# Decay, beta and running-maximum rows repeated over the partitions by GpSimd's transfers instead of by products with the identity

## Time and profile before

| | |
|---|---|
| median of three runs | 1260.62 us (1257.66 to 1260.63) |
| the profiled execution, its own time | 1257.48 us |
| its span, from first to last instruction | 1255.5 us |
| PE busy | 1183.1 us (94%) |
| DVE busy | 314.8 us (25%) |
| ACT busy | 129.1 us (10%) |
| POOL busy | 33.7 us (3%) |
| moved by DMA | 441.27 MB, mean 351 GB/s |
| the chain that ended last, by engine | PE 65%, DMA 31%, DVE 3% |

### The profile page before, as it was taken

The page is one execution under the profiler, slowest core; times in us unless marked ns, Lnnn a source line. Parts: engine busy times, 40 slices in busy tenths (PEclk is TensorE's granted clock), DMA queues, the critical chain, the costliest instruction groups (busy, mean ns, idle before and its releaser), DMA issues.

```text
span 1255.5 us, 13834 instructions
## 1 busy us (share of the span) xinstructions
PE 1183.1 (94%) x5889; PEld 623.5 (50%) x5889; DVE 314.8 (25%) x686; ACT 129.1 (10%) x216; POOL 33.7 (3%) x48
## 2 busy tenths in 40 slices
PE   8999999999999999999899898999999898899986
PEld 6889999985633443434334242434434243434342
DVE  2784325252520211102011110102111010202012
ACT  3551001101000000000000000000000000000001
POOL 3700000000000000000000000000000000000000
PEclk9999999999899999999999999999999999999999
DMA  9933323474699999999999999899999999999993
GB/s 269 328 101 107 105 91 109 176 300 187 253 430 416 428 428 428 427 429 426 427 430 426 428 427 418 360 428 427 429 428 426 428 428 426 429 427 427 429 428 146
DMA packets 61582, 441.27 MB, mean 351 GB/s; under 512 B 8176, under 2 KB 32976, under 8 KB 36848
## 3 DMA queue, kind: packets, MB, share of 16 engines
q1 hardware_dynamic: 57104, 438.38, 85.0%
q10 hardware_dynamic: 4416, 1.99, 0.7%
HBM read 439.30 MB, written 1.05 MB: 351 GB/s over the span
## 4 chain that ended last, share of the span: by engine, by line
PE 65%; DMA 31%; DVE 3%; issue 0%; SPq 0%; ACT 0%; DVEq 0%
DMA ring<-in_w_down 31%; PE bank L805 21%; PE bank L845 14%; PE bank L493 13%; PE bank L509 3%; PE bank L785 3%; PE bank L746 2%; PE bank L882 2%; PE bank L716 1%; PE bank L705 1%; PE bank L797 1%; PE bank L857 1%; PE bank L516 1%; PE bank L579 0%; DVE cvg L1440 0%; PE bank L867 0%
## 5 line engine op out<-in xcount | busy, mean ns | idle before, releaser
L805 PE MATMUL bank<-ring,cvg 128*64 128x512 f32 x2112 | 461.6, 593 | 9.0 <-DMA ring<-in_w_gate_up 8.7
L805 PEld LDWEIGHTS bank<-ring,cvg 128*64 128x64 f32 x2112 | 151.2, 137 | 300.2 <-issue 274.9
L845 PE MATMUL bank<-ring,cvg 128*64 128x512 f32 x1024 | 236.3, 618 | 38.7 <-DMA ring<-in_w_down 38.7
L1450 DVE TENSOR_SCALAR cvm<-bank 128x512 f32<-128x512 f32 x33 | 22.8, 691 | 654.8 <-PE bank L805 654.8
L845 PEld LDWEIGHTS bank<-ring,cvg 128*64 128x64 f32 x1024 | 80.6, 142 | 192.5 <-issue 192.4
L493 PE MATMUL bank<-ring 128*128 128x256 f32 x768 | 171.7, 382 | 0.0
L493 PEld LDWEIGHTS bank<-ring 128*128 128x128 f32 x768 | 145.4, 192 | 19.9 <-issue 0.7
L1801 ACT ACTIVATE cvm<-cvm 128x512 f32<-128x512 f32 x33 | 20.8, 630 | 501.7 <-DVE cvm L1450 501.7
L785 PEld LDWEIGHTS bank<-ltm,hn 128*128 128x128 f32 x544 | 67.8, 199 | 7.1 <-issue 7.1
L785 PE MATMUL bank<-ltm,hn 128*128 128x128 f32 x544 | 67.9, 284 | 0.0
L882 PE MATMUL bank<-vb,ltm 128*128 128x512 f32 x128 | 57.7, 593 | 0.0
(11 more groups left out here) (315 smaller groups left out, 615.1 us busy)
## 6 DMA issues: line engine op xcount, KB each, us to landing
ring<-in_w_gate_up SPq DMA_DIRECT2D x128, 2048.0 KB, 34.6
ring<-in_w_down SPq DMA_DIRECT2D x64, 2048.0 KB, 36.7
ring<-in_w_in SPq DMA_DIRECT2D x24, 1024.0 KB, 6.6
ring<-in_w_out SPq DMA_DIRECT2D x4, 1024.0 KB, 5.0
ring<-in_w_up_ml SPq DMA_DIRECT2D x2, 1024.0 KB, 5.1
ring<-in_w_up_gdn SPq DMA_DIRECT2D x2, 1024.0 KB, 5.0
xs<-in_x SPq DMA_DIRECT2D x2, 512.0 KB, 4.6
out<-hn SPq DMA_DIRECT2D x2, 512.0 KB, 2.7
```

Source lines behind the costliest of these rows:

```text
L805: mm = pe.matmul(B[4 + half][side * SLOTS:(side + 1) * SLOTS, :], xT[:, k, e * SLOTS:(e + 1) * SLOTS], w[:, (k % 2) * PIECE + at:(k % 2) * ...
L845: mm = pe.matmul(B[6 + half][e * SLOTS:(e + 1) * SLOTS, :], actT[:, e, at:at + SLOTS], by_block(double(of[e]), 4)[:, j, half * HALF:(half ...
L1450: dve.tensor_scalar(g2, both[:, :, :, 0], SWIGLU_LIMIT, None, ALU.min).then_inc(sem("glu_g_ready"), 1)
```

## The change

`spread` and its three calls are gone from PE. GpSimd gets a function of four transfers, `share_rows`, between its tables and the splitting of the bias: `rows` and `cmrow` are written to DRAM and read back to all 128 partitions, 8 KB and 4 KB on each. They land in parts of the ring of weights that are not in use then (`spread_rows` where the gates come later, `spread_runmax` where `inv` comes later). DVE reads its three operands there, in SBUF, instead of in PSUM, and waits for the transfers' semaphores.

```diff
--- before.py
+++ after.py
@@ -152,6 +152,10 @@
         cvm = sb("cvm", [P, 2 * HC, S])
         gate_g = ring[:, 9, 0:KC * S].rearrange("p (k s) -> p k s", k=KC)
         gate_m = ring[:, 9, KC * S:2 * KC * S].rearrange("p (k s) -> p k s", k=KC)
+        spread_rows = gate_g.rearrange("p (h b) s -> p h (b s)", b=1)
+        spread_runmax = late[4].rearrange("p (h s) -> p h s", h=H)
+        rows_copy = nc.dram_tensor("rows_copy", [2 * H, S], F32).ap()
+        runmax_copy = nc.dram_tensor("runmax_copy", [H, S], F32).ap()
         z_s, mo_s, mv_s = rows4(late[0]), rows4(late[1]), rows4(late[2])
         decay = mixer_only(T * H * P).rearrange("p (h t i) -> p h t i", h=H, t=T)
         pt = ring[:, 8, KC * S:KC * S + 3 * H * P].rearrange("p (h b i) -> p h b i", h=H, b=3)
@@ -459,6 +463,17 @@
                     link(ins)
             ins.then_inc(sem("tables_ready"), 1)
 
+            def share_rows():
+
+                pool.wait_ge(sem("rows_ready"), 1)
+                pool.dma_start(rows_copy, rows[:, :]).then_inc(sem("rows_kept"), 16)
+                pool.dma_start(runmax_copy, cmrow[:, :]).then_inc(sem("runmax_kept"), 16)
+                pool.wait_ge(sem("rows_kept"), 16)
+                pool.dma_start(spread_rows, rows_copy.partition_broadcast(P)).then_inc(sem("rows_spread"), 16)
+                pool.wait_ge(sem("runmax_kept"), 16)
+                pool.dma_start(spread_runmax, runmax_copy.partition_broadcast(P)).then_inc(sem("runmax_spread"), 16)
+
+            share_rows()
             pool.wait_ge(sem("expert_bias"), 48)
             for i in range(3):
                 own = slice(i * E, (i + 1) * E)
@@ -573,16 +588,6 @@
                 mm = pe.transpose(B[5][:, 480 + t * H:480 + (t + 1) * H], cmrow[:, t * P:(t + 1) * P], ident[0:H, 0:H])
             mm.then_inc(sem("runmax_turned"), 1)
 
-            def spread(src, first, banks, signal):
-                n = src.shape[0]
-                for h in range(H):
-                    mm = pe.matmul(B[banks[h // 2]][:, (h % 2) * S:(h % 2 + 1) * S],
-                                   ident[0:n, first + h:first + h + 1].to_broadcast([n, P]), src[:, :],
-                                   start=True, stop=True)
-                mm.then_inc(sem(signal), 1)
-
-            pe.wait_ge(sem("hT_ready"), 2 * T)
-            spread(rows, 0, (0, 1), "decay_spread")
             proj(4)
 
             pe.wait_ge(sem("squares_ready"), 2)
@@ -593,9 +598,6 @@
             mm.then_inc(sem("norm_sums"), 1)
             proj(5)
             pe.wait_ge(sem("roots_ready"), 2)
-            spread(rows, H, (2, 3), "beta_spread")
-            pe.wait_ge(sem("dmin_ready"), 1)
-            spread(cmrow, 0, (4, 5), "runmax_spread")
             proj(6)
 
             pe.wait_ge(sem("k_normed"), 1)
@@ -1146,10 +1148,10 @@
                                          op1=ALU.mult).then_inc(sem(done), 1)
 
             normed(0, 1, QS, "q_normed")
-            dve.wait_ge(sem("decay_spread"), 1)
+            dve.wait_ge(sem("rows_spread"), 16)
             for h in range(H):
                 for t in range(T):
-                    ins = dve.tensor_scalar(decay[:, h, t, :], B[h // 2][:, (h % 2) * S + t * P:(h % 2) * S + (t + 1) * P],
+                    ins = dve.tensor_scalar(decay[:, h, t, :], spread_rows[:, h, t * P:(t + 1) * P],
                                             rowsrc[:, t, h:h + 1], 0.0, ALU.subtract, ALU.min)
             ins.then_inc(sem("decay_log"), 1)
             conv(4)
@@ -1163,9 +1165,9 @@
                                      scalar=-1.0, in1=fcum[:, :, :], op0=ALU.mult, op1=ALU.subtract).then_inc(sem("dmin_ready"), 1)
             normed(HC, 2, 1.0, "k_normed")
             conv(5)
-            dve.wait_ge(sem("runmax_spread"), 1)
+            dve.wait_ge(sem("runmax_spread"), 16)
             for h in range(H):
-                src = B[4 + h // 2][:, (h % 2) * S:(h % 2 + 1) * S]
+                src = spread_runmax[:, h, :]
                 link(dve.tensor_scalar(pt[:, h, 0:2, :].rearrange("p b i -> p (b i)"), src, acol[:, 0, h:h + 1], 0.0,
                                        ALU.subtract, ALU.max))
                 ins = dve.tensor_scalar(pt[:, h, 2, :], src[:, P:S], acol[:, 1, h:h + 1], 0.0, ALU.subtract, ALU.max)
@@ -1178,8 +1180,7 @@
                 dve.wait_ge(sem("kk_done"), b + 1)
                 v = lt[:, 2 * b:2 * b + 2, :, :].rearrange("p h t i -> p (h t i)")
                 link(dve.tensor_tensor(v, B[b], decay[:, 2 * b:2 * b + 2, :, :].rearrange("p h t i -> p (h t i)"), ALU.mult))
-                dve.wait_ge(sem("beta_spread"), 1)
-                link(dve.tensor_tensor(v, v, B[2 + b], ALU.mult))
+                link(dve.tensor_tensor(v, v, spread_rows[:, H + 2 * b:H + 2 * b + 2, :].rearrange("p h s -> p (h s)"), ALU.mult))
             dve.wait_ge(sem("levels_ready"), len(LEVELS))
             l8 = lt[:, :, :, :].rearrange("p h t i -> p (h t) i")
             m8 = ltm[:, :, :, :].rearrange("p h t i -> p (h t) i")
```

## The result

The changed kernel is slower by half a per cent: 1269.32 us median (1264.40 to 1270.20, 13 runs) against 1261.86 us for the kernel before (1257.27 to 1263.98, 13 runs), a ratio of 1.0053 with an interval of 1.0039 to 1.0067. That is 7.5 us by the medians and 6.7 by the ratio, where 13.7 were forecast. The 13 runs fall into two groups, six from 1264.4 to 1267.3 us and seven from 1269.3 to 1270.2; only one run, of the second group, was traced, so what separates them stays open. The profiled execution took 1269.79 us, its span 1267.8.

What follows compares the result with a forecast made beforehand. PE's chain in the mixer was taken to bound, DVE just behind. Decay held by POOL until 78.0 us, plus 16.5, puts `proj(7)` at 94.5 instead of 80.84: 1260.6 + 13.7 = 1274.3, predicted 1274 us, range 1257 to 1280.

Steps and rivals of the forecast that it cites:

- S: When POOL is free of the transfers and starts splitting the bias: 51.1 us, with bounds of 48 and 59.
- the sum: Mixer: decay complete at 51.1 + 24.3 + 1.2 + 1.4 = 78.0 us, 16.5 more to `proj(7)` at 94.5.
- What bounds: Mixer: PE's chain bounds, DVE a few us behind; of 5.5 us of products removed, 3.5 us would be gained.
- the meeting: DVE's SBUF copies, two-input products and decay subtractions stand still until the POOL splitting instruction in progress ends, 51 to 75 us.
- When the rows are ready: End of DVE's scan, before the transfers: 46.2 us, less 1.3 us of waiting that goes, so 44.9.
- The price of POOL's transfers: Ahead of the splitting: 0.6 us per issue, 4.4 us for the small write, 6.6 us for the 1 MB read.
- The transfers in time: At DVE's decay, wanted at 58.63 us: the read lands at 57, just in time, or up to 4 us late.
- One for one: At the decay: the eight subtractions alternate with POOL's instructions, six each held by one; complete at 78.0 instead of 60.8 us.
- Passed on to the end: Behind `proj(7)`: its difference, 13.7 us, is the difference at the end; up to 1.8 us more for a lower clock.
- Rival A: At the decay: DVE keeps the port between back-to-back subtractions; 0 to 4 us slower, 1263 us; chance 0.20.
- B: Mixer: splitting runs beside DVE at little cost, transfers in time; gain 3.5 to 4 us, 1257 us; chance 0.17.
- C: At the decay: the read lands at 62 to 66 us and DVE stands 3.5 to 7.5 us; 1262 us; chance 0.13.

Runs made afterwards that it cites:

- the splitting first: Changed kernel, but POOL splits the bias first and issues the four transfers behind that: 1263.0 us, ratio 1.0008 to the kernel before.
- Linked subtractions: Changed kernel, but each of the eight decay subtractions waits until the one before it has written: 1272.9 us, ratio 1.0099 to the kernel before.
- the splitting late: Changed kernel, but POOL starts splitting the bias only at PE's first q.k product, near 106 us: 1257.0 us, ratio 0.9969 to the kernel before.
- two experiments: Changed kernel with POOL's splitting started near 106 us (1257.0 us), or with ACT issuing the transfers and the splitting at its old place (1258.1 us).
- products kept: Kernel before, with its spreading products and PSUM operands, plus the four transfers on POOL, whose copies nobody reads: 1264.3 us, ratio 1.0016.
- before with the splitting late: Kernel before with one edit, POOL starting the splitting of the bias near 106 us: 1260.5 us, ratio 1.0000.
- decay by products: Changed kernel with POOL's splitting near 106 us, but the decay spread by eight products and read from PSUM: 1257.4 us, ratio 0.9979 to before.

## Why the prediction was right, and where its size was off

- **The number.** 1269.3 us lies inside the stated range, which was wide (1257 to 1280), and just under the forecast's own, 1270 to 1281. At `proj(7)` the errors worked against each other: the later S added 1.5 us, the subtractions took 7.5 less than the sum had from S on, and the mask added 1.0. So 94.5 became 89.5.
- **What bounds.** Right: PE in the mixer, and DVE just behind it. With the meeting gone PE waits for DVE at `proj(6)`, the head products and `proj(7)`, for 3.4 us together, and gains 3.4 (3.5 expected).
- **When the rows are ready.** Right: the scan ended at 46.4 us, 44.9 without the late start, as the sum had it.
- **The price of POOL's transfers.** A little low. Issues took 0.70, 0.53, 0.57 and 0.54 us (0.6 taken), the write of 8 KB 5.5 us (4.4 taken), the read of 1 MB 7.6 (6.6 taken). S was 54.1, or 52.6 without the late start, instead of 51.1. (The 3 us that bounded a landing from below stand in no row shown.) The share of the DMA engines was 1.0 to 1.1 in these us. The Trainium skill, "DMA: Bandwidth & Descriptors", section "Anatomy of one DMA — SWDGE (gpsimd) path", has 2.0 us plus the bytes over 436 GB/s; as an estimate that is 4.4 us for the read, further from the 7.6 measured than my 6.6, and also under the 5.6 of the kernel with the splitting first.
- **The transfers in time.** Right: 0.29 us late with the splitting out of the way.
- **The meeting.** Right in kind: the moved splitting, the operands in SBUF, whole POOL instructions waited for. The product L1147 stood 3.2 us, of which I had counted 1.6, since S was later.
- **One for one.** This is the term that was mis-sized. In the case of the earlier trace rows POOL's instruction had been taken at 9.26 us, long before DVE took its next at 9.86. Here the second subtraction of a pair is taken as POOL's instruction ends, 0.05 to 0.1 us before POOL takes its next one, so it goes first. Four POOL instructions got in between eight subtractions and not six. They ended at 73.45, 72.0 without the late start, instead of 78.0; then 16.5 us and 1.0 for the mask, which met POOL because POOL was not through: 89.5, and 89.7 was measured. Linked subtractions, where one for one holds, gave 13.9 us at `proj(7)`.
- **Passed on to the end.** About right. The ratios give 6.7 us of the 9.0 here, 12.5 of 13.9 for the linked ones, and 3.9 for 3.4 with the splitting late. Why the slower kernels give 1 to 2 us back was not settled; the executions of one kernel differ by more than that, and each kernel has one trace.
- **Rival A** (the subtractions stay together) was half true, for two at a time. **B** is what two experiments made by taking the meeting away. **C** didn't decide.

## What to carry to other kernels

Work that is moved on one queue meets other work: the four transfers cost little, but they pushed 24 us of GpSimd's casts and subtractions beside the one place where VectorE had just been given its operands in SBUF. Before moving GpSimd work or turning a PSUM operand into an SBUF one, list VectorE's copies, subtractions of one operand and two-input products in SBUF there, and count instructions, not columns. And when products leave TensorE, look for the engine right behind it: here the waits for VectorE left 3.3 us of gain at `proj(8)`, and 6.4 once the order was changed too.

## What was not expected of the hardware

- GpSimd gets in once for every two VectorE instructions that follow without a wait (8 subtractions, 4 stands; 16, the same six POOL instructions as with 8 linked), and once for each when they are linked. In each of the stands looked at, the instruction that was taken first went first.
- The granted clock and products with 4 or 8 rows: the projection right behind them took 8.65 to 8.86 us instead of 7.07 in four kernels (before, products kept, before with the splitting late, decay by products), but not every time: `proj(4)` behind eight of them took 7.17 in the first three of these. Where they are gone and PE does not wait long, `proj(6)` took 7.15. That the few rows lower the clock is thus likely and not shown. The clock fell behind a long wait too: in the changed kernel the granted clock was 0.50, the lower level, from 69.5 us on, PE having stopped at 66.0, and `proj(6)` took 9.49 us. In all of these the loss at `proj(6)` fell into waits for DVE or was there before as well.
